# A block kernel on one NeuronCore: modulation sums on VectorE, second memory's values from whole slabs, layer norm two slabs later

## The reference

```python
# cross attention of layer l; m = rmsnorm(mem, norm_mem_g[l])
k, v = jnp.split(m @ wkv, 2, axis=-1)
# mixer of layer 0
yb = jax.nn.silu(layernorm(cv, ln_g, ln_b))
out = jnp.concatenate([ya, yb], axis=-1) @ w_out
# second block
cond = jax.nn.silu(c)                 # 1 x 1024
mod = cond @ w_ada[l] + b_ada[l]      # 1024 x 3072
shift, scale, gate = jnp.split(mod, 3, axis=-1)
h = rmsnorm_2(x, norm_g[l]) * (1.0 + scale) + shift
proj = h @ w_in[l]
x = x + gate * y
```

## Time and profile before

| | |
|---|---|
| three runs | 1748.06, 1749.21, 1750.06 us |
| profiled execution, span | 1746.6 us |
| PE busy | 1703.0 us, 97% |
| DVE busy | 1030.4 us, 59% |
| ACT busy | 710.7 us, 41% |
| mean granted PE clock | 0.994 |

### The profile page before, as it was taken

The page is one execution under the profiler, slowest core; times in us unless marked ns, Lnnn a source line. Parts: engine busy times, 40 slices in busy tenths (PEclk is TensorE's granted clock), DMA queues, the critical chain, the costliest instruction groups (busy, mean ns, idle before and its releaser), DMA issues.

```text
span 1746.6 us, 21516 instructions
## 1 busy us (share of the span) xinstructions
PE 1703.0 (97%) x8243; PEld 1379.1 (79%) x8243; DVE 1030.4 (59%) x1434; ACT 710.7 (41%) x1148; POOL 23.7 (1%) x44
## 2 busy tenths in 40 slices
PE   7999999999999999999999999999999999999998
PEld 6778888788888888887657878888888887887776
DVE  5799454456555543278875634755555346457695
ACT  6222432634333322235763453533333112156574
POOL 1000000000000000000100000000000000000000
PEclk9999999999999999999999999999999998999999
DMA  6277343222222223221002212222222322321201
GB/s 196 81 244 238 97 145 121 73 97 97 96 96 96 96 90 109 81 92 41 30 19 99 95 49 73 96 96 96 96 96 96 103 90 72 97 75 53 73 25 49
DMA packets 154293, 164.39 MB, mean 94 GB/s; under 512 B 2998, under 2 KB 150383, under 8 KB 153967
## 3 DMA queue, kind: packets, MB, share of 16 engines
q1 hardware_dynamic: 153408, 162.51, 28.6%
q0 software_dynamic: 336, 0.53, 0.2%
q10 hardware_dynamic: 479, 0.39, 0.1%
HBM read 160.01 MB, written 3.15 MB: 93 GB/s over the span
## 4 chain that ended last, share of the span: by engine, by line
PE 87%; DVE 6%; ACT 4%; issue 1%; DMA 1%; SPq 0%; DVEq 0%; ACTq 0%
PE bank L928 86%; ACT xa_p L1636 1%; ACT mla_p L1636 1%; DVE w_lo L2138 1%; DMA x_nat<-in_x_dram 1%; ACT w_hi L1636 1%; PE bank L1346 0%; DVE nmax L2628 0%; DVE h_lo L2138 0%; DVE mla_q L2603 0%; ACT fb L1636 0%; DVE xa_pT_lo L2138 0%; DVE cv L2248 0%; DVE mla_q L2589 0%; PE bank L1595 0%
## 5 line engine op out<-in xcount | busy, mean ns | idle before, releaser
L928 PE MATMUL bank<-h_hi,w_hi 128*128 128x512 f32 x1472 | 579.7, 394 | 6.9 <-DVE w_lo L2138 2.7
L928 PE MATMUL bank<-h_hi,w_lo 128*128 128x512 f32 x1472 | 574.0, 390 | 0.0
L928 PE MATMUL bank<-h_lo,w_hi 128*128 128x512 f32 x1472 | 573.7, 390 | 0.0
L2138 DVE TENSOR_TENSOR w_lo<-w_raw,w_hi 128x2048 fp32r<-128x2048 f32 (+4 forms) x142 | 286.0, 2018 | 281.9 <-ACT w_hi L1636 281.6
L1636 ACT ACTIVATE w_hi<-w_raw 128x2048 fp32r<-128x2048 f32 (+4 forms) x142 | 239.2, 1689 | 381.2 <-PE bank L928 375.7
L928 PEld LDWEIGHTS bank<-h_hi,w_hi 128*128 128x128 f32 x1472 | 276.6, 188 | 72.9 <-issue 10.4
L928 PEld LDWEIGHTS bank<-h_hi,w_lo 128*128 128x128 f32 x1472 | 276.5, 188 | 58.5
L928 PEld LDWEIGHTS bank<-h_lo,w_hi 128*128 128x128 f32 x1472 | 276.8, 188 | 57.8 <-issue 1.2
L928 PE MATMUL bank<-g_hi,w_hi 128*128 128x512 f32 x352 | 136.9, 389 | 0.0
L928 PE MATMUL bank<-g_lo,w_hi 128*128 128x512 f32 x352 | 136.9, 389 | 0.0
L928 PE MATMUL bank<-g_hi,w_lo 128*128 128x512 f32 x352 | 136.9, 389 | 0.0
(11 more groups left out here) (372 smaller groups left out, 2038.3 us busy)
## 6 DMA issues: line engine op xcount, KB each, us to landing
w_raw<-in_ffn_w_up_dram SPq DMA_DIRECT2D x44, 1024.0 KB, 5.0
w_raw<-in_ffn_w_down_dram SPq DMA_DIRECT2D x16, 1024.0 KB, 5.1
w_raw<-in_w_in_dram SPq DMA_DIRECT2D x13, 1024.0 KB, 5.2
w_whole<-in_xa_wkv_dram SPq DMA_DIRECT2D x12, 1024.0 KB, 5.5
w_whole<-in_w_ada_dram SPq DMA_DIRECT2D x12, 1024.0 KB, 7.6
w_raw<-in_xa_wq_dram SPq DMA_DIRECT2D x8, 1024.0 KB, 5.2
w_raw<-in_xa_wo_dram SPq DMA_DIRECT2D x8, 1024.0 KB, 5.1
w_raw<-in_pc_w_in_dram SPq DMA_DIRECT2D x6, 1024.0 KB, 5.5
```

Source lines behind the costliest of these rows:

```text
L928: return nc.tensor.matmul(o, w, v, start=start, stop=stop, **kw)
L2138: return tt(lo_, v, hi.bitcast(f32), SUB)
```

## The change

Three edits. `ada` is no stage any more: the loads of its twelve slabs stand in the second down projection, two at a time, and DVE multiplies each 256-column piece by the condition's column for it and adds it to `ada_acc`. PE's part is 24 column sums around the spread of the norm; `mod` and `gs2` are made there. All of `kv1` is whole. The layer norm's sums stand behind `kv1` slabs 5 and 6, Sqrt and the four Silu behind slab 6, ahead of the last `kv_out`; the first `pc_out` slab is loaded and split early, all of it waits for `kv_free` 32, and it is multiplied in two halves of its rows. The first `wo0` slab is split in `wq0`.

```diff
-STAGES = [("pc_in", 6), ("kv0", 8), ("kv1", 8), ("ada", 12), ("pc_out", 4), ...
+STAGES = [("pc_in", 6), ("kv0", 8), ("kv1", 8), ("pc_out", 4), ...
 def whole(n):
-    return stage in ("ada", "kv0") or stage == "kv1" and s < 4
+    return ORDER[n][0] in ("kv0", "kv1")
+EARLY = [AT["pc_out", 0], AT["pc_out", 1]]
+LOADS[LOADS.index(WHOLE_SLABS[ROUND - 6]):LOADS.index(WHOLE_SLABS[ROUND - 6])] = EARLY
+        ADA_AT = (1, 3, 5, 7, 9, 10)
...
 # SP
+            def load_ada(pair):
+                sp.wait_ge(slab_half, 2 * FIRST["down1"])
+                wait(sp, ada_added, 2 * DT * pair)
+                for i in range(2):
+                    src = ...
+                    sp.dma_start(view(ada_w[i], DT, 256), src).then_inc(ada_loaded[i], 16)
...
+                for pair, s in enumerate(ADA_AT):
+                    if n == FIRST["down1"] + max(s + 1, 2):
+                        load_ada(pair)
...
 # PE, memory stage
             for s in range(8):
                 memory(0, s)
-                for u in ada_behind(s):
-                    ada_row(u)
-                    if u:
-                        ada_columns(u - 1)
-            ada_columns(ADA_FIRST - 1)
...
             for s in range(8):
-                (memory if s < 4 else lambda layer, s: memory_values(s))(1, s)
+                memory(1, s)
                 if s == 0:
                     mix_pooled((2, 3))
-                if s == 2:
+                if s == 5:
                     pe.wait_ge(y_lo, 4)
                     ...                                   # sum over cv
-                if s == 3:
+                if s == 6:
                     ...                                   # sum over the squares
-            pe.wait_ge(kv_free, 30)
-            linear("pc_out", (y_lo, 0), lambda s: pe.wait_ge(kv_free, 32) if s == 0 else None)
-            pe.wait_ge(mod_done, 1)
+            pe.wait_ge(lo_done, splits_before(n) + 1)
+            pe.wait_ge(kv_free, 32)
+            for k0 in (0, 4):
+                for j in range(2):
+                    slab_tile("pc_out", n, j, ..., 4, ..., ready=(y_lo, k0) if j == 0 else None, first=k0 == 0, last=k0 == 4, ...)
+            for s in range(1, 4):
+                slab("pc_out", FIRST["pc_out"] + s, ...)
...
 # PE, cross attention of layer 0
-                    if layer == 0:
-                        ada_row(ADA_FIRST + h)
                     outputs(h)
-                    if layer == 0 and h:
-                        ada_columns(ADA_FIRST + h - 1)
...
 # PE, behind the second down projection
+            def ada_columns(part):
+                pe.wait_ge(ada_added, DT * ADA)
+                for c in range(DT * part, DT * (part + 1)):
+                    m = mm(ada_sum[part][:, c:c + 1], ada_acc[:, c * P:(c + 1) * P], ones[:, 0:1], True, True)
+                m.then_inc(ada_cols, 1)
+            ada_columns(1)
             spread(bank[6], fb[0], 3 * NB)
+            ada_columns(0)
+            ada_columns(2)
...
 # ACT, kv1
                 kv_out(1, s)
-                if s in (1, 3, 4, 5):
-                    split(AT["kv1", {1: 4, 3: 5, 4: 6, 5: 7}[s]])
-                if s == 2:
+                if s == 5:
                     ...                                   # squares
+                    split(FIRST["pc_out"])
-                if s == 3:
+                if s == 6:
                     act.wait_ge(xc_summed, 4)
                     ...                                   # Sqrt
-                if s == 4:
                     ...                                   # four Silu
-                if s == 6:
-                    split(FIRST["pc_out"])
...
 # DVE, second down projection
+                def add_ada(pair):
+                    for i in range(2):
+                        dve.wait_ge(ada_loaded[i], 16 * (pair + 1))
+                    for k in range(DT):
+                        for i in range(2):
+                            u = 2 * pair + i
+                            o, v = ada_acc[:, u * 256:(u + 1) * 256], ada_w[i][:, k * 256:(k + 1) * 256]
+                            if k == 0:
+                                m = ts(o, v, c_silu[:, 0:1], None, MUL)
+                            else:
+                                dve.wait_ge(ada_added, 2 * (DT * pair + k - 1) + i + 1)
+                                m = stt(o, v, c_silu[:, k:k + 1], o, MUL, ADD)
+                            m.then_inc(ada_added, 1)
                 for s in range(12):
                     split(n + s + 1)
+                    if s in ADA_AT:
+                        add_ada(ADA_AT.index(s))
                     if s % 3 == 2:
...
 # DVE, norm of the second block, behind the diagonals of the spread
+            dve.wait_ge(ada_cols, 1)
+            modulation(1).then_inc(mod_done, 1)
+            ...                                           # gs2 from it, two operations
             dve.wait_ge(stat2_done, 2)
             for i in range(DT + 1):
                 if i < DT:
                     ...                                   # line 2712
+                if i == 0:
+                    dve.wait_ge(ada_cols, 2)
+                    modulation(0).then_inc(mod_done, 1)
+                    dve.wait_ge(mod_done, 2)
+                if i == 3:
+                    dve.wait_ge(ada_cols, 3)
+                    modulation(2).then_inc(mod_done, 1)
                 if i:
                     ...                                   # line 2715
```

More of the change, by code:

```diff
@@ L45 @@
 SLAB = 2048
-STAGES = [("pc_in", 6), ("kv0", 8), ("kv1", 8), ("ada", 12), ("pc_out", 4), ("wq0", 4), ("wo0", 4), ("up0", 22),
+STAGES = [("pc_in", 6), ("kv0", 8), ("kv1", 8), ("pc_out", 4), ("wq0", 4), ("wo0", 4), ("up0", 22),
           ("down0", 12), ("dq", 3), ("ukv", 2), ("uq", 4), ("mla_o", 4), ("wq1", 4), ("wo1", 4), ("up1", 22),
@@ L51 @@
 COUNT = dict(STAGES)
[L57 to L67, removed]
+ADA = 12
+ORDER = [(_name, _s) for _name, _count in STAGES for _s in range(_count)]
 AT = {_slab: _n for _n, _slab in enumerate(ORDER)}
@@ L132 @@
 DQ_TILES = (2, 3, 4, 5, 0, 1)
-TILES = {"ada": 0, "kv0": 0, "kv1": 0, "down0": 8, "down1": 8, "ukv": 16, "uq": 12, "w_out": 16}
+TILES = {"kv0": 0, "kv1": 0, "down0": 8, "down1": 8, "ukv": 16, "uq": 12, "w_out": 16}
 TILE0 = {}
@@ L371, in build @@
         mem_sums, mem_col = nmax[:, 0, 0:2], nmax[:, 1, 0:2]
[L373 to L377, removed]
+        ada_sum = [bank[5], bank[4], bank[(TILE0["w_in"] + 3) % 4]]
         def sem(name):
@@ L392, in build @@
         csilu_done = sem("csilu_done")
-        ada_copied = sem("ada_copied")
+        ada_loaded = [sem(f"ada_loaded{i}") for i in range(2)]
+        ada_added = sem("ada_added")
         ada_cols = sem("ada_cols")
@@ L1239, in cross @@
                 cross_attention(layer)
[L1240 to L1245 removed]
+                linear(f"wo{layer}", (xo_lo, 8 * layer))
                 ffn(layer)
@@ L1881, in cross @@
                         a(h_hi[:, 2 * h + d, :], x_out(layer, d)[:, :], ACT.Copy).then_inc(xo_hi, 1)
-                    if layer == 0 and h == 1:
-                        split(FIRST["wo0"])
                 splits_and_norm(f"wo{layer}", f"ffn{layer}")
@@ L2315, in _ @@
             conv(len(todo))
-            for i in range(DT):
-                dve.wait_ge(m1_done, DT + i + 1)
-                low(m1_lo[:, i, :], m1[:, i, :], m1_hi[:, i, :]).then_inc(mem_lo, 1)
-            split(AT["kv1", 4])
             dve.wait_ge(cv_summed, 4)
@@ L2323, in _ @@
                 stt(cv[:, i, :], bank[4][:, :], -1.0 / (4 * P), cv[:, i, :], MUL, ADD).then_inc(xc_ready, 1)
-            split(AT["kv1", 5])
+            split(FIRST["pc_out"])
             dve.wait_ge(ln_sqrt, 1)
@@ L2328, in _ @@
                 tt(cv[:, i, :], cv[:, i, :], rstd[:, :], MUL).then_inc(ln_norm, 1)
-            split(AT["kv1", 6])
-            split(AT["kv1", 7])
-            split(FIRST["pc_out"])
             for i in range(4):
```

109 lines of the change are left out of this document (26 added, 83 removed).

## The result

| | before | after |
|---|---|---|
| median of 10 runs each, us | 1749.82 (1745.37 to 1750.39) | 1754.31 (1753.34 to 1755.57) |
| ratio after / before | | 1.0027, 95% interval 1.0019 to 1.0035 |
| profiled execution: span, us | 1746.6 | 1752.0 (its time 1753.89) |
| mean granted clock in it | 0.994 | 0.989 |

A forecast was written before the change was run, and what follows sets the result against it. PE, busy 97%, was taken as the bound, with waits for DVE and ACT operands; 2.0 + 4.0 - 7.4 + 0.7 + 5.9 = +5.2 us gives span 1751.8, time 1754.4, range 1748 to 1759.

The forecast's parts named there:

- The two waits: Memory stage: PE stands 6.5 us ahead of the third pool matmul and 4.4 us ahead of pc_out; stage +2.0 without clock.
- T: Memory stage: when PE reaches the sum over the squares, forecast 204.6 us, before 190.55; pc_out's wait is counted from it.
- The clock behind them: Memory stage: PE's clock falls to 0.50 behind each wait, 2.0 us each, 4.0 together; bounds 0 and 3.4 each.
- The attention: First cross attention, scores to second x addition of wo0: 51.25 us becomes the other layer's 43.88, -7.4; bounds -6.6 and -8.
- bound of -6.6: First cross attention: the smaller gain, taken as the price of four modulation rows with columns on a full PE.
- The second down projection: DVE's added sums at 0.35 us an operation, 33 us in all, mostly fit beside PE: +0.7 us, bounds 0 and 3.
- The margin at s = 5: Second down projection, tightest place: DVE's next w_lo at 1407.0, PE needs it at 1408.26; holds by 1.3 us.
- rival 4: Second down projection: DVE late from 0.43 us an operation, norm starts 5 us late; +11, 1760 us; 11%.
- The tail: Norm behind the second down projection: 24 columns at clock 0.50 delay the spread 1.7 and w_in 4.2 more: +5.9 us.
- Rival 2: Clock stays up in both waits and through the tail's columns, 1.7 us a group: -5.8, 1743.4 us; 7%.
- w_in starting 12 to 14 us after the last down matmul: Tail: a sign that was to show the forecast right, the gap on PE from last down matmul to w_in.
- over 3 us: Tail: a sign that was to show the forecast right, each column group on PE lasting over 3 us.

The follow-up runs named there:

- e2: Changed kernel with pc_out's first slab waiting only for kv_free 30, and kv_free 32 asked for ahead of its second slab; 1748.37 us, 0.9987 of before.
- e1: Changed kernel with DVE making the low parts of mixer tiles 0 and 1 ahead of ten convolution taps; 1747.20 us, 0.9983 of before.
- e8: Kernel before with the first cross attention's four modulation rows cut to two matmuls over 16 columns and one short column; 1748.97 us, ratio 0.9986.
- e10: Changed kernel with four extra 128x1536 products on DVE ahead of the third pair's sums in the second down projection; 1760.99 us, 1.0052 of before.
- e4: Changed kernel without the modulation product: no loads, DVE sums or PE columns, modulation is the bias alone; 1746.90 us, 0.9983 of before.
- a0: The changed kernel itself, run again beside the kernel before; 1754.61 us, 1.0033 of before.
- e6: Changed kernel with low parts ahead of taps, the later kv_free 32 wait, and 20 columns moved into down1; 1738.54 us, 0.9939 of before.
- e7: Changed kernel with low parts ahead of taps and the later kv_free 32 wait, columns left in the tail; 1743.85 us, 0.9958 of before.
- e3: Changed kernel with 20 of the 24 modulation columns summed on PE between slabs of the second down projection; 1753.60 us, 1.0027 of before.
- e5: Kernel before with the first cross attention's four modulation rows cut to two matmuls of 32 rows each; 1749.28 us, ratio 0.9997.
- e9: Changed kernel with only the 24 columns on PE left out, modulation the bias alone, loads and DVE sums kept; 1750.12 us, 0.9997 of before.

## Why the prediction was right, and where only in sum

**The two waits.** Both are where they were put, at 6.43 for 6.5 us and 3.97 for 4.4. The trace names DVE's h_lo for the first; for the second it names nobody, and e2 shows that it is the copies of xa_v. e1 got back 8.3 us at pc_out where the forecast had added 8.5, e2 7.0 by its ratio for 6.4. pc_out started at T + 14.66 for T + 14.7.

**The clock behind them** was taken at 2.0 us each. The first cost 2.0, the second 3.0. e1 shows that the second figure isn't a property of the wait: there the same 3.96 us were followed by 3.4 us at 0.50 instead of 6.8.

**The attention** is -7.4 to the tenth, since the other layer was an honest twin. The working behind its bound of -6.6 was wrong: that was the price of four rows and columns on a full PE, but e8 puts the rows at 3.1 here, PE's waits behind the early split of wo0 make up 1.9, and 1.7 us of the gain were a stretch at 0.50 in the kernel before that the forecast didn't look for.

**The second down projection.** The operation was taken at 0.35 us; 14 of them take 5.63, that is (5.63 - 0.48) / 13 = 0.40 start to start, 0.48 being how long one lasts. The forecast said that none of this kind stands in the trace of before, but the same operation does at 512 columns: the taps of the earlier trace rows last 0.74 each and start every (6.70 - 0.74) / 9 = 0.66 us, the TENSOR_TENSOR of the earlier trace rows every (2.49 - 0.68) / 3 = 0.60. This kind costs 0.06 more; with the subtractions of the earlier trace rows at (2.77 - 0.42) / 7 = 0.34 start to start, that makes 0.40. The margin at s = 5 is 0.6 us and not 1.3, the last pair lands 8.3 us after its issue (1437.80) and not 7.9, and the end is 1.3 late and not 0.7. The bounds (0.3 to 0.5) held, rival 4 (from 0.43 on) was 0.03 us away, and e10 shows that lateness of DVE beyond the margin costs PE nearly one to one. The Trainium skill (VectorE: DVE Perf Modes, The TRN2 errata) states (N + 151) / 0.96 ns for an fp32 tensor_tensor add, by estimate 0.424 us at 256 columns. That agrees with how long one of the subtractions lasts (0.42), not with how soon the next one starts (0.34), and the operation of `add_ada` is another one.

**The tail.** The column groups took 2.92 and 6.83 us for 2.9 and 6.8, the spread started 1.5 us later against the sums (forecast 1.7), w_in 8.5 behind the spread (8.7). The term was too large by 1.0 us: 0.4 in these two, and 0.6 since the dense matmuls of w_in stood at 0.50 for only 3.1 us, where before it was 4.3. Rival 2's full-clock columns didn't come. The sign "w_in starting 12 to 14 us after the last down matmul" failed, and it never fitted the forecast's own sum: the last down matmul starts at 1455.83, w_in 15.5 us later, and 8.8 in the kernel before plus 0.7 and 5.9 would have been 15.4. The first column group, at 2.92, was also just under the "over 3 us" of the signs, as its own term of 2.9 had it.

**Not in the forecast:** +1.2 at the start, where the first memory slab begins anywhere from 87.0 to 91.0 us in the thirteen profiles of this study, and -1.7 in the latent attention, 3.4 us at 0.50 for 6.8. Neither place was changed; the latter stretch (second x addition to down1) takes 979.1 to 985.6 us in the thirteen profiles. That the sum is right to 0.2 us is luck: +1.2, +1.0 behind the second wait, +0.6 in down1, -1.7, and -1.0 in the tail cancel. That every changed place came within 1.0 us, term by term, isn't.

**The table load.** In the trace of after, the activation starts 1.29 us after its table load began, as in the earlier trace rows, and the load began right behind the activation ahead of it (212.16 + 0.64 = 212.80, 212.81); the 1.38 us more by the Trainium skill (ScalarE: Activation LUTs, What ACT_TABLE_LOAD costs) are not there.

## What to carry to other kernels

Work taken from a full PE is worth its time only up to the next operand that another engine has in its queue behind something longer: before moving such work, list for each engine the last thing that it does ahead of what PE will ask for next, and move that thing too (e1 and e2 are a few lines, and by the ratios 12 us together). A wait should name only what the next instruction writes or reads. One-column work is cheaper among dense matmuls (0.95 us a group of four columns) than in the norm's chain (2.92 and 6.83 us for 8 and 16 columns), but the time of the kernel showed that only beside e1 and e2.

## What the runs showed of the hardware

**The clock decides as much as the work.** Over the 35 runs of the kernel before beside e1 to e4, time and mean granted clock go together (correlation -0.96, about 1.4 us for each 0.001), and within each kernel of the eleven experiments too (-0.64 to -0.97). The median over the runs of time times clock is 1738.8 us for before and 1736.2 for a0. By this rough measure, which takes every stretch at 0.50 as work at half rate, also where PE waits, the changed kernel has no more to do than the one before, and its lower clock makes it slower; the lower clock comes in good part from the change itself, for 13.7 us at 0.50 stand behind the two new waits. For e6 the measure is 1728.1, for e7 1727.2, whose median is 5.3 us higher at 0.990 for 0.994.

**What lengthens the stretch at 0.50 in the tail.** In the profiles without the 20 to 24 columns there it lasted 6.8 us (e4, e6) or 10.2 (before, e3, e5, e8, e9); with them 13.7 (after, e2, e10), 17.1 (a0) and 20.5 (e1, e7). In these six PE was busy for nearly all of the stretch (10.50 of 10.50 us in the kernel after, 18.00 of 18.00 in e7): one-column matmuls back to back didn't hold the clock, and dense ones stood at 0.50 for up to 6 us behind them. In e3 groups of 8 such records among dense matmuls didn't bring it down. Which of the three lengths comes is open; the code of the tail is the same in all six.

**Side by side.** Sixteen records of 32-row matmuls in four places of the array take 1.07 us, four records in one place 1.05. A count of records is no measure of PE time there.
